# A transformer and state-space block on one core: where the tensor `work`, and the split rows under it, begin in the on-chip memory

## What is computed

```python
act = jax.nn.gelu(jnp.einsum("nd,nhkd->nhk", hb, ue).astype(jnp.float32))
return jnp.einsum("nhk,nhkd->nd", (g * act).astype(hb.dtype), ve)
```

## Time and profile before

| | before |
|---|---|
| median of 3 runs | 3909.91 us |
| span of the profiled execution, first to last instruction | 3906.2 us |
| TensorE matmul busy | 3797.3 us (97%) |
| VectorE busy | 2874.6 us (74%) |
| ScalarE busy | 1607.4 us (41%) |
| mean granted TensorE clock | 0.987 |

### The profile page before, as it was taken

The page is one execution under the profiler, slowest core; times in us unless marked ns, Lnnn a source line. Parts: engine busy times, 40 slices in busy tenths (PEclk is TensorE's granted clock), DMA queues, the critical chain, the costliest instruction groups (busy, mean ns, idle before and its releaser), DMA issues.

```text
span 3906.2 us, 61715 instructions
## 1 busy us (share of the span) xinstructions
PE 3797.3 (97%) x21514; PEld 3167.1 (81%) x21514; DVE 2874.6 (74%) x5194; ACT 1607.4 (41%) x2462; POOL 88.1 (2%) x101
## 2 busy tenths in 40 slices
PE   8999999999999999999999999999979999999998
PEld 8896798557977888888888888888748888888887
DVE  7533275996988799999887777776565997777776
ACT  5301152233147444444494444444332194444443
POOL 0000000000000000000000000000400000000000
PEclk9999999999999999999999999999979999999999
DMA  5314454575434555555515555555765515555554
GB/s 197 100 57 149 148 200 149 170 227 184 136 114 152 197 193 193 191 193 189 193 60 195 190 188 190 188 188 204 176 220 177 167 60 194 190 188 191 188 188 151
DMA packets 203775, 666.32 MB, mean 171 GB/s; under 512 B 35920, under 2 KB 46176, under 8 KB 202480
## 3 DMA queue, kind: packets, MB, share of 16 engines
q1 hardware_dynamic: 166816, 602.47, 46.7%
q0 software_dynamic: 12496, 52.53, 4.3%
q10 hardware_dynamic: 24320, 9.37, 0.9%
HBM read 637.10 MB, written 26.15 MB: 170 GB/s over the span
## 4 chain that ended last, share of the span: by engine, by line
PE 89%; DVE 8%; DMA 1%; ACT 1%; issue 1%; SPq 0%; DVEq 0%; ACTq 0%
PE psum L1117 27%; PE psum L1103 17%; PE psum L1105 9%; PE psum L719 5%; PE psum L1196 5%; PE psum L744 4%; PE psum L659 4%; PE psum L1291 3%; PE psum L1387 2%; PE psum L1185 2%; PE psum L780 1%; DVE arena L2473 1%; PE psum L1083 1%; DMA ring<-in_w 1%; DVE arena L2474 1%; PE psum L1162 1%
## 5 line engine op out<-in xcount | busy, mean ns | idle before, releaser
L1117 PE MATMUL psum<-rows_split_odd,coef_split 128*128 128x512 f32 x2400 | 589.0, 395 | 3.6 <-DVE rows_split_odd L2617 3.6
L2622 DVE TENSOR_REDUCE work<-psum 128x256 f32<-128x512 f32 x360 | 248.9, 691 | 387.5 <-PE psum L1105 386.6
L1117 PE MATMUL psum<-rows_split,coef_split 128*128 128x512 f32 x2208 | 532.1, 390 | 0.3 <-issue 0.3
L1117 PEld LDWEIGHTS psum<-rows_split_odd,coef_split 128*128 128x128 f32 x2400 | 436.7, 188 | 104.6 <-issue 6.9
L1103 PE MATMUL psum<-input_split,rows_split 128*128 128x512 f32 x1440 | 513.9, 397 | 1.2 <-ACT arena L1583 1.2
L1794 ACT ACTIVATE work<-work 128x256 f32<-128x256 f32 x360 | 150.7, 419 | 876.7 <-DVE work L2622 876.7
L1103 PE MATMUL psum<-input_split,rows_split_odd 128*128 128x512 f32 x1440 | 510.0, 393 | 0.0
L2617 DVE TENSOR_TENSOR rows_split_odd<-ring,rows_split_odd 128x1024 fp32r<-128x1024 f32 x380 | 462.2, 1217 | 8.9 <-ACT rows_split_odd L1583 8.9
L1117 PEld LDWEIGHTS psum<-rows_split,coef_split 128*128 128x128 f32 x2208 | 402.0, 188 | 81.5 <-issue 0.9
L1583 ACT ACTIVATE rows_split_odd<-ring 128x1024 fp32r<-128x1024 f32 x380 | 400.5, 1055 | 155.8 <-PE psum L1117 153.7
L2617 DVE TENSOR_TENSOR rows_split<-ring,rows_split 128x1024 fp32r<-128x1024 f32 x364 | 442.7, 1216 | 5.4 <-ACT rows_split L1583 5.4
(11 more groups left out here) (466 smaller groups left out, 5370.8 us busy)
## 6 DMA issues: line engine op xcount, KB each, us to landing
ring<-in_u SPq DMA_DIRECT2D x384, 512.0 KB, 3.3
ring<-in_v SPq DMA_DIRECT2D x384, 512.0 KB, 3.2
ring<-in_w SPq DMA_DIRECT2D x372, 512.0 KB, 3.5
scratch_inj<-stage ACTq DMA_DIRECT2D x16, 512.0 KB, 5.5
arena<-scratch_inj POOLq DMA_DIRECT2D x7, 1024.0 KB, 8.4
scratch_cm<-work POOLq DMA_DIRECT2D x8, 512.0 KB, 5.9
scratch_cm<-arena POOLq DMA_DIRECT2D x8, 512.0 KB, 5.0
arena<-scratch_parked POOLq DMA_DIRECT2D x4, 1024.0 KB, 7.8
```

What stands on the lines that cost most here:

```text
L1117: last = mm(bank(2 + 2 * i + f), CFR[:, b, c, P * i:P * i + P], parts[:, v, 512 * f:512 * f + 512], start=(first and c == 0 and v == 0), s ...
L2622: dve.tensor_reduce(AC[:, b, :], bank(b).rearrange("p (x t) -> p t x", x=2), AX, ALU.add)\
```

## The change

The allocation of `small` moves behind that of `work`, and the block that names `rows_split_odd` is with `work` as before. `work` and `rows_split_odd` move down by 3280 bytes per partition, to the end of `stage`. `small` moves up by 20672 bytes, which is 10 times 2048 and 192 more, a multiple of 64. `tail` and `extra` stay where they were. No engine's list of instructions changes in number, order or waits; the addresses of operands do.

```diff
         stage = sb("stage", [P, 1024])
-        small = sb("small", [P, NCOLS])
         with nc.sbuf_tensor("rows_split_odd", [P, 2, 2, SLOT], F32R) as t:
             SPLB = t[:, :, :, :]
         work = sb("work", [P, 5120 + 48])
+        small = sb("small", [P, NCOLS])
         tail = sb("tail", [P, 576])
```

## The result

The median went from 3909.64 us to 3924.49 us (4 runs each, 3918.29 to 3926.44 after). The medians differ by 14.9 us, 0.38%; the ratio of the runs is put at 1.0032, with a 95% interval from 1.0021 to 1.0044. I had forecast 3901 us, so the sign was wrong, and the time lies beyond the range. The profiled execution has a span of 3916.5 us, 10.3 above that of before.

A forecast was written before the change was run, and what follows sets the result against it. TensorE's matmuls in the sweeps were taken to bound the kernel. Downs -12.0 and ups +3.6 gave -8.4 us on a span of 3906.2, so 3897.8 and a median of 3901 us; range 3887 to 3910.

The forecast's parts named there:

- A sweep is a pure TensorE stage.: Sweeps over the experts: matmuls busy 709.46 of 710 us, so only what they gain or lose lies on the path.
- Columns of the downs: L1117 on `rows_split_odd`: 200 downs, each from 2.79 to 2.73 us once their columns are aligned, 12.0 us less.
- Weights of the ups: L1103 on the odd tensor: 180 ups, each from 2.79 to 2.81 us with aligned weights, 3.6 us more.
- My picture of 64-byte blocks: Matmul columns on `rows_split_odd`: 2048 bytes starting 16 off a multiple of 64 touch 33 blocks, not 32; gap 6.5 ns.
- Rivals 1 and 2: 1: not alignment but tensor's place, gap stays, 3909.9 us, chance 0.17; 2: all ups settle at 2.77 us, 3887, chance 0.15.
- VectorE, ScalarE, one-hot matrices, `small`: Work beside the sweeps' matmuls, gate matmuls L1196 and the load of `small`: no change, the load bounded by -0.9 and +0.9 us.
- Rival 3: Sweeps: aligned weights and columns hinder each other, ups 2.88 us, +16.8 us, 3927; decides above 2.83 us an up; chance 0.08.
- The bounds: Limits of the downs' and ups' terms, combined to -23 us and, with nothing gained on the downs, +3.6 us.
- rival 2: Sweeps: all ups settle at 0.347 us a pair, 2.77 us each; with the downs 22.8 us less, 3887; chance 0.15.

The follow-up runs named there:

- gap16: Changed kernel with 16 bytes (rounded to 32) between `stage` and `work`, putting `rows_split_odd` off a multiple of 64 again; 3910.07 us, beside 3908.96 for the kernel before.
- the scan: Sweep loop in a program of TensorE alone, 16 offsets of the ups' weights by 8 of their columns, both sides alike; periods from 11.00 to 11.214 us.

## Why the prediction was wrong, point by point

- **"A sweep is a pure TensorE stage."** Right: the whole difference of the profiles lies in the sweeps (+12.7 us), with no idle time in them.
- **Columns of the downs, -12.0 us.** This is the step that failed, in two ways. The 200 downs on the odd tensor were to go from 2.79 to 2.73 us; they went to 2.783, over the 180 periods -1.6 us. And a term was missing: the downs on the *even* tensor, with no address changed, went from 2.728 to 2.783 us, 180 x 0.055 = +9.9 us. I took the even down's 2.73 us for a property of aligned columns. It was a property of its place in the loop, behind an up with misaligned weights, and the change removed just that. The rows said so in part: the earlier trace rows has a down on `rows_split` behind an up on `rows_split_odd`, and there was no row of an aligned down behind an aligned up. The downs in the earlier trace rows, which I used as a proof, come behind other downs. There the forecast did come true: in the third sweep's opening, where downs on the odd tensor follow one another, most matmuls start 226.7 ns apart after the change and some 234 before, and the whole row is shorter (before, then after):

```profile
3216.50 22.63 PE L1117 MATMUL psum<-rows_split_odd,coef_split 128*128 128x512 f32 x96 [0.56 <-DVE rows_split_odd L2617]
3223.36 22.37 PE L1117 MATMUL psum<-rows_split_odd,coef_split 128*128 128x512 f32 x96 [0.56 <-DVE rows_split_odd L2617]
```

- **Weights of the ups, +3.6 us.** Right to the nanosecond: 2.810 us on both sides, 180 x 0.02 us. Here I had asked what stands in front, and copied a case with nearly the same predecessor. It was in part luck: the down in front of the copied up took 2.728 us and those in front of the new ones take 2.783, and behind a down with the columns of before the same aligned up takes 2.816. The same question about the down behind it would have found the error.
- The two, corrected: -1.6 + 9.9 + 3.6 = +11.9 us, against 11.3 and 12.7 us in the sweeps of two profiles. In the profile after, 8 matmuls of the second sweep's opening started 426 ns apart, at a mean granted clock of 0.72 in this window, so that part of it ran at the 1.2 GHz level; the profile before has none such there. At 200 ns each, they add 1.6 us.

```profile
2050.00:2056.00 6.00, 5.17 (x16) 4.17 (x17) 3.93 (x8) 1.24 (x2) 0.00 (x0) 0.72 0.58 197
```

- **My picture of 64-byte blocks.** Wrong in its ground (the tensor was 32 bytes off, not 16) and in its rule: columns 64 bytes off cost 2.3 ns as well, and weights that are off by the same 64 cancel it.
- **Rivals 1 and 2** fell: the period changed with the offset and not with the place (gap16), and no up of the changed kernel's loop reached 2.77 us.
- **VectorE, ScalarE, one-hot matrices, `small`.** Right at nothing: the split's rows stayed at 1217 and 1054 ns and L1196 at 279, and the load of `small` takes 6.01 us in place of 6.13. The span outside the sweeps differs from before by -2.4 us in one profile and -11.0 in the other, so it scatters by 9 us between profiles of the same kernel.
- **Rival 3 (slower, 0.08)** had the sign and near enough the time (3927), not the mechanism, so that its number was luck. The ups stayed at 2.81 us, below its deciding point of 2.83; the downs were what slowed down. I had its observation in hand, that the aligned up is the slow one, and gave it 0.08 because the aligned down was fast.
- The range held nothing on the slow side beyond no change, though the forecast rested on a difference of 5 ns whose cause I had only inferred. The bounds were added up wrongly as well: with nothing gained on the downs and the odd ups at their own bound of 2.88 us, the two terms give 180 x 0.09 = +16.2 us, not +3.6, and the measured loss lies within that; on the fast side they give -14.0 - 3.6 = -17.6, and the -23 is the sum of rival 2, with the even ups faster too.

What stays open is what inside TensorE makes the rhythm. The periods found in the scan stand 13.3 ns apart (11.000, 11.013, 11.027, 11.040, ...), which is 32 columns at 2.4 GHz. The runs show that the offsets of weights and of columns matter together and up to 256 bytes, but not through what port or buffer.

## What to carry to other kernels

Where TensorE streams back to back, read the distance between starts, and compare a matmul only with one that has the same predecessors; a fast neighbour can be fast because of what runs before it. Alignment is no good in itself: with every operand aligned this loop was among the slowest of the 128 offsets tried. A program of TensorE alone reproduces such a loop to a nanosecond, so offsets or an order of the matmuls can be chosen there, and the addresses in the built program should be read before a theory is built on them.

## What was not expected of the hardware

- A stream of fp32r matmuls of 512 columns, each with its own weight load, settles between 226.7 and 236.7 ns with the operands' offsets alone (236.7 with the columns 4 bytes off); one of 256 columns between 113.3 and 123.3. The 113.3 ns come with the weights 64 bytes off, where 512 columns take 233.3: the best offset for one width isn't the best for the other.
- An alternating stream of 512 and 256 columns has two stable steps, 0.347 and 0.353 us a pair, at one and the same addresses, and which one sets in depends on what ran before it. In the kernel before, the even up behind the second sweep's opening has pairs of 350 and 343 ns in turn, and the even ups of the steady loop have pairs of 349, 350 and 361, in 178 of 180 ups. The steady loop keeps the slower one from the second pair to the last.
- In single streams and in the loop, offsets of 0 and 256 bytes behave alike, 64 and 128 don't.
